# A two-block transformer on one core: where the weight splits stand among the eviction parts of the second block's feed-forward

## What is computed

```python
D_FF = ((8 * D_MODEL // 3 + 127) // 128) * 128      # 2816
...
def causal_dwconv(u, w):                             # three taps along the tokens, per feature
    ...
    for l in range(DEPTH):
        ...
        h = rmsnorm(x, norm_ffn_pre[l])
        u = h @ w_up[l]
        ua, ub = u[..., :D_FF], u[..., D_FF:]
        y = (jax.nn.silu(causal_dwconv(ua, conv_ffn_w[l])) * ub) @ w_down[l]
        x = x + rmsnorm(y, norm_ffn_post[l])
```

## Time and profile before

| | |
|---|---|
| runs before | 1940.62, 1946.37, 1950.4 us (median 1946.37) |
| the profiled execution's own time | 1939.84 us |
| its span in the trace | 1938.0 us |
| TensorE busy | 1775.3 us (92%) |
| VectorE busy | 1201.8 us (62%) |
| ScalarE busy | 903.2 us (47%) |
| granted TensorE clock, mean | 0.964 |
| second block's feed-forward, layer 0, `ub1` to the end of `down0` | 1154.57 to 1312.88 us of the span |
| the same, layer 1 | 1720.74 to 1879.44 us of the span |

### The profile page before, as it was taken

The page is one execution under the profiler, slowest core; times in us unless marked ns, Lnnn a source line. Parts: engine busy times, 40 slices in busy tenths (PEclk is TensorE's granted clock), DMA queues, the critical chain, the costliest instruction groups (busy, mean ns, idle before and its releaser), DMA issues.

```text
span 1938.0 us, 31984 instructions
## 1 busy us (share of the span) xinstructions
PE 1775.3 (92%) x13736; PEld 1691.8 (87%) x13736; DVE 1201.8 (62%) x1626; ACT 903.2 (47%) x1275; POOL 331.3 (17%) x128
## 2 busy tenths in 40 slices
PE   6998999999989999999998889869899998898877
PEld 6877999998769999998998789869898998798877
DVE  4765576546655765459657656673658577566663
ACT  5464544444655444533535554444434436544442
POOL 5520200045212000135021010001162022000000
PEclk9988999999999999999999999989998999999989
DMA  6320555544205555544344334444443344344441
GB/s 249 102 79 15 185 185 181 168 171 132 66 28 184 181 177 181 194 148 154 122 147 158 131 126 148 151 131 164 160 149 129 131 164 153 119 147 147 138 143 63
DMA packets 52413, 276.28 MB, mean 143 GB/s; under 512 B 5936, under 2 KB 6320, under 8 KB 51888
## 3 DMA queue, kind: packets, MB, share of 16 engines
q1 hardware_dynamic: 51984, 272.14, 41.4%
q10 hardware_dynamic: 288, 2.10, 0.3%
HBM read 273.16 MB, written 1.05 MB: 141 GB/s over the span
## 4 chain that ended last, share of the span: by engine, by line
PE 67%; DVE 20%; ACT 8%; issue 4%; DMA 0%; POOL 0%; SPq 0%; DVEq 0%; ACTq 0%
PE bank L736 14%; PE bank L739 13%; PE bank L738 13%; DVE weights_lo L622 6%; ACT weights_hi L611 4%; DVE conv L1999 2%; PE scores L736 2%; PE scores L739 2%; PE scores L738 2%; PE scores L1244 2%; PE bank L1384 1%; PE heads L736 1%; PE heads L738 1%; PE heads L739 1%; PE turned L1236 1%
## 5 line engine op out<-in xcount | busy, mean ns | idle before, releaser
L622 DVE TENSOR_TENSOR weights_lo<-raw,weights_hi 128x1536 fp32r<-128x1536 f32 (+1 forms) x278 | 482.7, 1756 | 322.6 <-ACT weights_hi L611 322.3
L611 ACT ACTIVATE weights_hi<-raw 128x1536 fp32r<-128x1536 f32 (+3 forms) x352 | 498.9, 1439 | 192.5 <-PE bank L739 106.4
L736 PE MATMUL bank<-x_hi,weights_lo 128*128 128x256 f32 (+1 forms) x1808 | 524.2, 290 | 17.3 <-DVE weights_lo L622 9.5
L738 PE MATMUL bank<-x_lo,weights_hi 128*128 128x256 f32 (+1 forms) x1808 | 514.4, 285 | 0.0
L739 PE MATMUL bank<-x_hi,weights_hi 128*128 128x256 f32 (+1 forms) x1808 | 514.2, 284 | 0.0
L635 POOL TENSOR_TENSOR weights_lo<-raw,weights_hi 128x1536 fp32r<-128x1536 f32 (+4 forms) x74 | 256.1, 3477 | 1085.2 <-ACT weights_hi L611 1085.0
L736 PEld LDWEIGHTS bank<-x_hi,weights_lo 128*128 128x128 f32 (+1 forms) x1808 | 347.8, 192 | 28.0 <-DVE weights_lo L622 11.2
L738 PEld LDWEIGHTS bank<-x_lo,weights_hi 128*128 128x128 f32 (+1 forms) x1808 | 347.8, 192 | 2.3 <-issue 2.0
L739 PEld LDWEIGHTS bank<-x_hi,weights_hi 128*128 128x128 f32 (+1 forms) x1808 | 347.6, 192 | 0.0
L736 PE MATMUL bank<-hidden_hi,weights_lo 128*128 128x256 f32 x704 | 200.9, 285 | 25.2 <-DVE hidden_lo L2022 23.4
L738 PE MATMUL bank<-hidden_lo,weights_hi 128*128 128x256 f32 x704 | 200.0, 284 | 0.0
(11 more groups left out here) (337 smaller groups left out, 3327.5 us busy)
## 6 DMA issues: line engine op xcount, KB each, us to landing
raw<-in_w_b SPq DMA_DIRECT2D x194, 768.0 KB, 4.3
raw<-in_w_a SPq DMA_DIRECT2D x122, 768.0 KB, 4.4
raw<-in_w_a SPq DMA_DIRECT2D x14, 512.0 KB, 3.6
raw<-in_w_b SPq DMA_DIRECT2D x10, 512.0 KB, 4.5
mem<-in_mem ACTq DMA_DIRECT2D x2, 1024.0 KB, 4.8
raw<-in_w_a SPq DMA_DIRECT2D x2, 752.0 KB, 4.4
raw<-in_w_b SPq DMA_DIRECT2D x2, 752.0 KB, 4.1
raw<-in_w_b SPq DMA_DIRECT2D x2, 720.0 KB, 5.6
```

What stands on the lines that cost most here:

```text
L611: nc.scalar.activation(whi[c % SPLIT][:, 0:n], raw[c % RAW][:, 0:n], ACT.Copy).then_inc(*s.mark("weights_hi", c))
L622: nc.vector.tensor_tensor(wlo[c % SPLIT][:, 0:n], raw[c % RAW][:, 0:n], whi[c % SPLIT][:, 0:n].bitcast(F32), ALU.subtract).then_inc(*s.mar ...
L736: ins = nc.tensor.matmul(dst, wl, xh, start=start, stop=False, skip_group_check=skip)
L738: nc.tensor.matmul(dst, wh, xl, start=False, stop=False, skip_group_check=skip)
```

## The change

The list of the stage is written in another way, and two kinds of step are new to it. `own_splits` names the jobs whose step no longer issues splits on ScalarE and VectorE. `("chunks", (a, b))` makes VectorE's splits up to chunk a and ScalarE's up to chunk b. The four parts of pair i-1 now stand together behind the jobs of pair i, with one `chunks` step behind each of the first three parts. The products, the convolution and all instructions of each kind stay the same in number and shape; TensorE's sequence is the same.

```diff
-                    ("job", "ua0"), ("adds", "n3"), ("job", "ub0"), ("mean", "n3"), ("job", "ua1"), ("factor", "n3"),
-                    ("ffn_in", 0), ("job", "ub1"), ("ffn_taps", 0)]
-        for i in range(2, KF2 // 2):
-            order_b += [("job", f"ua{i}"), ("ffn_out", i - 2), ("ffn_in", i - 1), ("job", f"ub{i}"), ("ffn_lo", i - 2), ("ffn_taps", i - 1)]
+                    ("job", "ua0"), ("adds", "n3"), ("job", "ub0"), ("mean", "n3"), ("job", "ua1"), ("factor", "n3")]
+        done = jobs_b["ua1"].tiles[-1][-1][1] + 2
+        for i in range(1, KF2 // 2):
+            end = jobs_b[f"ub{i}"].tiles[-1][-1][1] + 2
+            first, second = min(done + 1, end), min(done + 2, end)
+            order_b += ([("job", f"ua{i}")] if i > 1 else []) + [("job", f"ub{i}"), ("ffn_in", i - 1), ("chunks", (first, second)),
+                        ("ffn_taps", i - 1), ("chunks", (second, end)), ("ffn_out", i - 1), ("chunks", (end, end + 1)), ("ffn_lo", i - 1)]
+            done = end
         n = KF2 // 2 - 1
-        order_b += [("ffn_out", n - 1), ("ffn_in", n), ("ffn_lo", n - 1), ("ffn_taps", n), ("ffn_out", n), ("ahead", f"ub{n}"), ("ffn_lo", n)]
+        order_b += [("ffn_in", n), ("ffn_taps", n), ("chunks", (done + 1, done + 1)), ("ffn_out", n), ("ffn_lo", n)]
...
+        own_splits = {f"{u}{i}" for i in range(1, KF2 // 2) for u in ("ua", "ub")} - {"ua1"}
...
                 elif kind == "job":
-                    split_hi(pl, act, l, pl.last_chunk(name) + 2)
+                    if name not in own_splits:
+                        split_hi(pl, act, l, pl.last_chunk(name) + 2)
...
+                elif kind == "chunks":
+                    split_hi(pl, act, l, name[1])
...
+                elif kind == "chunks":
+                    split_lo(pl, dve, l, name[0])
...
                 elif kind == "job":
-                    split_lo(pl, dve, l, pl.last_chunk(name) + 2)
+                    if name not in own_splits:
+                        split_lo(pl, dve, l, pl.last_chunk(name) + 2)
```

## The result

The changed kernel takes 1882.88 us (median of four runs, 1877.36 to 1886.28) against 1944.07 us for the kernel before (1940.62 to 1950.40): a ratio of 0.9679, 95% interval 0.9643 to 0.9715. So some 62 us are gone by the ratio, where 67 were forecast.

The account below looks back on a forecast made before the run. VectorE's round of 14.07 us a pair, against TensorE's 11.39, was taken as the bound. The profiled 1939.84 us less 66.8 is 1873.0; adding half the 6.5 us by which the median run lies higher gave 1876 us, range 1864 to 1892.

Parts of the forecast that it names:

- The bound and the rule of the wait: In the second feed-forward VectorE's round, 14.07 us a pair, sets the pace; its two waits for ScalarE's rounding take 4.43 us.
- One pair: VectorE's round per pair becomes 10.20, 10.20 and 9.30 us, 9.90 on average, under TensorE's 11.39.
- The tightest place of the walk: Early in the stage, chunk 67's low part is ready at 1168.6 and TensorE opens it at 1168.8, margin 0.2 us.
- The end of the stage: Pair 10's first hidden_lo comes at 1269.7 and TensorE reaches its features at 1269.9, a margin of 0.2 us.
- The sum: Each stretch from ub1 to down0 takes 124.1 us, 1044 products at 0.1186; 68.8 us saved, less 2 for slips, 66.8.
- one of the signs that the prediction had named for being wrong: TensorE's products coming slower than 0.1186 us while nothing waits would show the forecast wrong.
- The clock's share: Gain beyond the 26.3 us of waiting in each layer, put down to stalls lowering TensorE's clock, 0.59 after one 2.26 us stall.
- No hand-over that costs TensorE anything stayed: Rival: one wait between VectorE and ScalarE stays at 2.2 us, 20 us less won, about 1896; chance 0.09.
- it does what it says: Rival: VectorE waits for ScalarE for a reason other than order, time within 0.5%, 1946; chance 0.03.
- The loads followed: Rival: the stage's loads can't follow; at 161 GB/s 32 us of the gain go, 1908; chance 0.03.
- the slower rival: ScalarE's extra rounding blocks tap 2 until TensorE opens a chunk; at a 14.8 us round 15 us slower, 1961; chance 0.03.
- The rule of 109.2 ns per product: Skill's rule for warm 256-column TensorE products: 9.9 us less in each layer, time about 1856; chance under 0.01.

Follow-up runs that it names:

- the lead alone: Kernel before, old order of steps, with ScalarE rounding one chunk further ahead in jobs ua and ub: 1878.52 us, 1884.47 in a second measurement.
- the variant with the splits in one place: Changed kernel with all splits of a pair behind the first part, ScalarE still rounding one chunk ahead: 1897.93 us, ratio 0.9755 to the kernel before.

## Why the prediction was right

**The bound and the rule of the wait.** Right. The stretch was paced by VectorE's round with two waits for a rounding; the lead alone removes both, and without it the new order is slower than the old. After the first pair VectorE still waits for high parts at times in both, but then ScalarE has itself been waiting for TensorE to free a buffer.

**One pair.** 9.90 us was forecast for VectorE's round in the mean, 10.20 with three splits and 9.30 with two. Three rounds in a row in the changed kernel, before waits for a free buffer set in, take 10.22, 10.11 and 9.23 us, 9.85 in the mean. The tightest place of the walk came as forecast: chunk 67's low part at 1168.6 in the time of the first trace, and in the changed kernel at 1176.06 + 1.76 less the 9.26 us by which its stage began later, 1168.56.

**The end of the stage.** The walk left 0.2 us between `hidden_lo` of pair 10 and the product that reads it. It is 0.34: the first instruction runs from 1279.70 for some 0.42 us, and the product starts at 1280.46, the twenty-first block of a `down0` whose first stands at 1273.34:

```profile
1273.34 0.28 PE L736 MATMUL bank<-hidden_hi,weights_lo 128*128 128x256 f32 x1
...
1280.46 0.28 PE L736 MATMUL bank<-hidden_hi,weights_lo 128*128 128x256 f32 x1
```

The margin held although both of its ends came later than in the walk, counted from `ub1`'s start: pair 10's first part by 1.2 us (1271.74, 107.9 us in, where 106.7 was forecast) and the product by 1.3. Pair 9's last parts stand behind roundings that wait for TensorE, so slower products move both.

**The sum.** The two stretches gave 32.93 and 33.32 us, 66.3 together; the sum said 68.8, less 2 for slips, 66.8. That 66.3 lies so near to 66.8 is luck: two errors cancel. There were no slips (0 of the 2 us). And the step 0.1186 us per product, taken from `down1`, doesn't hold for the 912 products of the `ua` and `ub` jobs: they take 1273.34 − 1163.83 = 109.51 us, 0.1201 each, 1.3 us more a layer than forecast. This was one of the signs that the prediction had named for being wrong, and it cost little. The 60 us window of the first block's feed-forward, whose timeline has a product every 0.120 us, had said so (119.5 ns), and I put it down to missing records; in fact a window also counts the products in flight at its edges.

**The clock's share.** 32.9 us is more than the 26.3 of stall in layer 0. The prediction put all that is beyond the stall down to the clock; this step was sized wrong. Of the other 6.6 us a part is lost at every stall, at full clock. A stall in the middle of the stretch before, in TensorE's timeline and in a window:

```profile
1208.17 0.39 PE L736 MATMUL bank<-x_hi,weights_lo 128*128 128x256 f32 x1 [1.63 <-DVE weights_lo L622]
```

```profile
1201.96:1208.17 6.21, 4.58 (x37) 4.38 (x37) 4.10 (x8) 3.38 (x3) 0.00 (x0) 1.00 0.39 127
```

From 1201.96 to 1208.17 TensorE makes one chunk's 36 products, 4.32 us at 0.120, and waits 1.63; 0.26 us are left. The rows show where they go: the last product before a stall runs for its 0.28 us, where otherwise the next would start after 0.12, and the first one behind it is followed after 0.22 us (1201.96 and 1202.18) instead of 0.12. Layer 0 has 11 stalls, which makes about 2.8 us. The other 3.8 are slow products. The granted clock of the stretch was 0.95, so about a tenth of it, 15.8 us, ran at 1.2 GHz; now it is 1.00. By the Trainium skill, "TensorE: Matmul & The Clock Gate", section "Terms", the loss is about the throttled time times one half, an estimate of 7.9 us. The trace agrees only once the throttled time in which no product runs is left out, which is the last stall above all:

```profile
1294.97:1302.64 7.67, 0.00 (x0) 0.00 (x1) 4.76 (x8) 4.81 (x5) 0.00 (x0) 0.50 0.00 0
```

Half of the other 8.1 us is 4.1.

**The whole time.** 1876 was forecast, 1882.88 came, 6.9 us more. By 0.5 us the stretches gave less than the sum's 66.8. 1.3 us are the level: the kernel before lies at 1944.07 in the measurement beside the changed one, and 1876 plus 66.8 is 1942.8. The other 5.1 us the changed kernel lost outside the stretches, where no order changed: the medians lie 61.2 us apart, the stretches explain 66.3. Its traces take 1624.2 to 1633.7 us there, those of the kernel before 1620.6 to 1623.5, and the variant with the splits in one place 1617.1, which is most of why it came in under its range. The lower clock between 500 and 600 us (table above) is of this size; why it comes isn't settled. The intervals of both ratios still hold 66.3 us, so a part may be noise.

**The rivals.** No hand-over that costs TensorE anything stayed, and VectorE's waits did go with the order, so that it does what it says. The loads followed, at 184 GB/s. ScalarE's roundings do wait for a buffer in front of tap 2 and the tanh, as the slower rival had it, up to 2.4 us at a time, and TensorE has no stall in either stretch. The rule of 109.2 ns per product is out: 120.1 and 118.6 ns at full clock.

## What to carry to other kernels

When two engines hand work back and forth in fixed orders, look at what each does right after a hand-over: a piece that the partner needs next must have been made one turn earlier, and here one turn was enough. Moving pieces between the parts without that lead adds a wait at each place and can turn a gain into a loss; with the lead it only shortens the end. Try the lead alone first: here one number brought the stage from 158.5 to 127.0 us a layer, and the whole rewritten order to 125.4.

## What the runs showed of the hardware

**Products of one shape start at two rates at full clock.** In the changed kernel 132 products of a `down` job take 15.66 us (118.6 ns each), 912 of the `ua` and `ub` jobs 109.51 us (120.1 ns), both with 128x128 weights and 256 columns, TensorE never idle, clock 1.00. The Trainium skill, same page, section "Wait — 56ns, not 53.3ns?", would have both at 109.2 ns. The rate doesn't belong to the kind of job alone. With ScalarE's lead alone, `down1` of layer 0 takes 15.84 us, 120.0 ns a product, as its two ends on ScalarE show:

```profile
1289.90 0.60 ACT L1950 ACTIVATE squares<-bank 128x512 f32<-128x512 f32 x1 [5.65 <-PE bank L739]
...
1305.74 0.60 ACT L1950 ACTIVATE squares<-bank 128x512 f32<-128x512 f32 x1 [4.21 <-PE bank L739]
```

It does so in both traces of that kernel, while `down1` of layer 1 takes 15.66 in both. Of the 28 layers in the 14 traces five have the slower `down` jobs, one of them in the kernel before. No run here tells what makes the difference.

**The granted clock of a stage can differ from kernel to kernel though its own order is the same.** The windows from 500 to 600 us, in the first block's attention, in the first trace of the changed kernel:

```profile
500.00:600.00 100.00, 88.33 (x556) 72.86 (x555) 53.76 (x128) 54.70 (x126) 21.77 (x7) 0.85 0.13 43
```

and in the first trace of the kernel before:

```profile
500.00:600.00 100.00, 87.04 (x616) 73.60 (x615) 57.30 (x130) 56.68 (x129) 21.04 (x7) 0.95 0.19 64
```

The order of instructions there is the same; the granted clock is 0.85 and 0.95, and 60 more products fit into the second. The two further traces of the kernel before have 0.95 again, the three of the changed one 0.85, 0.85 and 0.86. The stretches without stalls took 125.38 us all eight times.
